# One inference step with retention and experts: the sample tokens' halves in one operand, and their state work placed later in the next head

## What is computed

```python
h = rmsnorm(x, g_mix)
z = h @ w_in                       # 1024 x 4608
u, q, k, v, ga, gb = split(z)      # 512 | 512 | 512 | 1024 | 1024 | 1024
pool_out = windowed mean of u per group, minus u, then w_pool
qf, kf = rotary(q), rotary(k) * 128 ** -0.5
# retention, 4 heads, dk 128, dv 256, chunks of 128 tokens:
#   o = (q k^T * decay) v + (q s) * xi ;  s = g_chunk * s + (k * zeta)^T v
# a sample token is a chunk of one: s_new = gamma * s + k v^T, o = q s_new
mixed = sigmoid(ga) * pool_out + sigmoid(gb) * head_group_norm(ret)
x = x + mixed @ w_out
x = x + hier_moe(rmsnorm(x))       # 32 experts, top 2
y = rmsnorm(x, g_final)
```

## Time and profile before

| | us |
|---|---|
| median of 3 runs | 1100.17 |
| lowest, highest | 1098.19, 1101.92 |
| the profiled execution | 1098.83 |
| its span, first to last instruction | 1096.6 |
| busy: TensorE, its weight loads | 1011.7, 861.0 |
| busy: VectorE, ScalarE, GpSimd | 757.9, 442.1, 203.7 |

### The profile page before, as it was taken

How to read it: one execution, slowest core, us unless ns; L and a number is a source line. 1 busy time by engine, 2 the same in 40 slices (tenths; PEclk the granted TensorE clock), 3 DMA queues, 4 the chain that set the end, 5 groups by cost and what they waited for, 6 DMA issues and landing times.

```text
span 1096.6 us, 17147 instructions
## 1 busy us (share of the span) xinstructions
PE 1011.7 (92%) x5426; PEld 861.0 (79%) x5427; DVE 757.9 (69%) x1846; ACT 442.1 (40%) x733; POOL 203.7 (19%) x227
## 2 busy tenths in 40 slices
PE   5799999999999999999998999958999999999970
PEld 4798888988789888898885888847888777878760
DVE  5675556755557565675556666678999889888955
ACT  6421113011130211301112222136888878978864
POOL 0001220012200122001220000012442322332420
PEclk9899999999999999999998999978999999999995
DMA  8511016010160100701007433289999999999728
GB/s 262 199 29 59 10 38 183 19 59 11 40 190 11 51 19 25 205 12 38 32 19 255 160 154 117 97 348 356 361 383 388 383 384 344 365 378 359 259 27 316
DMA packets 74735, 190.36 MB, mean 174 GB/s; under 512 B 12503, under 2 KB 47555, under 8 KB 62227
## 3 DMA queue, kind: packets, MB, share of 16 engines
q1 hardware_dynamic: 61403, 159.66, 39.5%
q0 software_dynamic: 13248, 29.62, 9.7%
HBM read 167.43 MB, written 38.68 MB: 188 GB/s over the span
## 4 chain that ended last, share of the span: by engine, by line
PE 64%; DMA 23%; DVE 6%; issue 4%; ACT 1%; SPq 1%; POOLq 0%; DVEq 0%; ACTq 0%; POOL 0%
DMA sum_d<-y,icol 19%; PE bank L1790 18%; PE bank L1791 9%; PE bank L848 8%; PE bank L821 5%; PE bank L823 5%; PE bank L822 5%; PE bank L877 1%; PE bank L1813 1%; PE bank L1805 1%; PE bank L1801 1%; PE bank L1685 1%; PE bank L1809 1%; DMA hc<-const_head_tables_dram 1%; PE bank L1677 1%
## 5 line engine op out<-in xcount | busy, mean ns | idle before, releaser
L1194 DVE TENSOR_TENSOR w_lo<-w,w_hi 128x1024 fp32r<-128x1024 f32 x128 | 150.5, 1217 | 0.4 <-DVE vec L1157 0.2
L711 ACT ACTIVATE w_hi<-w 128x1024 fp32r<-128x1024 f32 x128 | 129.4, 1067 | 4.1 <-PE bank L823 4.1
L1790 PE MATMUL bank<-wvg_hi,hT_hi 128*128 128x512 f32 x288 | 117.3, 407 | 0.4 <-DVE kT L1982 0.4
L1790 PE MATMUL bank<-wvg_lo,hT_hi 128*128 128x512 f32 x288 | 113.6, 394 | 0.0
L1790 PE MATMUL bank<-wvg_hi,hT_lo 128*128 128x512 f32 x288 | 113.3, 393 | 0.0
L1638 ACT ACTIVATE v<-bank 128x256 f32<-128x256 f32 x36 | 13.8, 382 | 233.5 <-PE bank L1791 233.5
L821 PE MATMUL bank<-w_hi,xT_hi 128*128 128x512 f32 x256 | 103.6, 405 | 3.3 <-issue 1.4
L823 PE MATMUL bank<-w_hi,xT_lo 128*128 128x512 f32 x256 | 101.0, 394 | 0.0
L822 PE MATMUL bank<-w_lo,xT_hi 128*128 128x512 f32 x256 | 100.5, 393 | 0.0
L821 PE MATMUL bank<-hT_hi,wuqk_hi 128*128 128x344 f32 x288 | 95.9, 333 | 2.7 <-issue 1.8
L2092 POOL TENSOR_TENSOR mixed<-onorm,pgate 128x256 f32<-128x256 f32 x36 | 36.1, 1004 | 314.5 <-DVE onorm L1938 314.5
(11 more groups left out here) (231 smaller groups left out, 2339.5 us busy)
## 6 DMA issues: line engine op xcount, KB each, us to landing
w<-in_w_dram SPq DMA_DIRECT2D x96, 1024.0 KB, 9.3
raw<-in_w_in_dram SPq DMA_DIRECT2D x60, 256.0 KB, 3.3
xall<-in_x_prompt_dram SPq DMA_DIRECT2D x8, 512.0 KB, 6.2
mixed_d<-mixed POOLq DMA_DIRECT2D x32, 128.0 KB, 2.2
sample_state<-in_state_ret_dram SPq DMA_DIRECT2D x16, 256.0 KB, 3.9
out_dram<-sample_state SPq DMA_DIRECT2D x16, 256.0 KB, 3.7
mixed_in<-mixed_d SPq DMA_DIRECT2D x8, 512.0 KB, 4.3
x_again<-in_x_prompt_dram SPq DMA_DIRECT2D x8, 512.0 KB, 3.4
```

What stands on the lines that cost most here:

```text
L711: act.activation(hi, whole_w, ACT.Copy).then_inc(S["up_hi"], 1)
L1194: dve.tensor_tensor(lo, whole_w, hi, ALU.subtract).then_inc(S["up_lo"], 1)
L1790: g = pe.matmul(gates, x[xi], wvg[wi][:, 1:3, k, :], start=first, stop=last)
```

## The change

- `hs`, a new tile, holds for each of eight k-slices the samples' high part at column 88 and the low part at column 120 of a window of 128 columns; windows start 20 columns apart, so other slices' values fall on unused columns. Chunk 8 takes one such window as stationary operand against high and low weights: two pairs of matmuls a slice for three. Rows 88 to 95 of the result (high) and 120 to 127 (low) are then added on VectorE, for v and for the gates.
- The outer products: k is transposed from `kw`, four copies of the last 32 columns; `ks` has k's low part in rows 32 to 63 and its high part in the others, `vs` has v's low part in rows 0 to 31 and high parts in the others, and `kblk` has 128 rows, all in fp32r. One fp32r matmul of 128 rows sums the parts.
- TensorE's loop over heads 1 to 3 is written out.
- The samples' work starts at n = 1 (outer products 0, 1), goes on at n = 3 (pooling product, read 0, outer product 2), n = 4 (read 1, outer product 3), n = 5 and 6 (reads 2 and 3). VectorE updates groups 0 and 1 behind the first three pieces, group 2 behind the rotation of n = 3, group 3 behind that of n = 4; the last three pieces go behind n = 5, the samples' norm behind n = 6 and n = 7.
- SyncE loads pieces 6 to 8 ahead of the wait for the state, and stores and loads sample states in another order among the pieces.

```diff
+HSTEP = 20
+HS = 120 + HSTEP * KT
...
-    m[:, KMASK:KMASK + NB] = i[:, None] == 120 + np.arange(NB)[None, :]
+    m[:, KMASK:KMASK + NB] = i[:, None] % 32 == 24 + np.arange(NB)[None, :]
...
+        def sample_cols(which):
+            at = 88 + 32 * which
+            return hs[:, at:at + HSTEP * KT].rearrange("p (k n) -> p k n", k=KT)[:, :, 0:NB]
...
             def tail(h, between):                      # SyncE
                 between(0)
+                sp.wait_ge(S["state_new"], after(8 * h + 8))
+                carried(sp, "sp")
+                sp.dma_start(ret_p[0, 0, bass.ds(h, 1)].rearrange("a d v -> (a d) v"), state[:, :])\
+                    .then_inc(st_out, 16)
+                between(1)
                 store_states(h, 0)
-                between(1)
                 store_states(h, 1)
+                between(2)
                 load_states(h, 2)
-                between(2)
                 load_states(h, 3)
                 between(3)
...
                     if c < CH:                         # ScalarE
                         act.activation(vb[c % 2][:, :], banks[2 + c % 2][:, 0:DV], ACT.Copy).then_inc(S["v_ev"], 1)
...
+                    else:
+                        act.activation(vs[64:P, :], banks[2][64:P, 0:DV], ACT.Copy)
+                        act.activation(vs[32:64, :], banks[2][64:Q3, 0:DV], ACT.Copy).then_inc(S["v_ev"], 1)
+                        act.wait_ge(S["gates_sum"], after(h + 1))
+                        act.activation(sg[0][Q3:P, :], sg[0][Q3:P, :], ACT.Sigmoid).then_inc(S["sig_done"], 1)
...
-                        mm = pe.matmul(banks[2 + g % 2][:, i * DV:(i + 1) * DV], kblk[Q3:P, 2 * g + i, :],
-                                       vb[0][Q3:P, :], start=True, stop=True)
+                        mm = pe.matmul(banks[2 + g % 2][:, i * DV:(i + 1) * DV], kblk[:, 2 * g + i, :], vs[:, :],
+                                       start=True, stop=True)
...
-                if n == 0:
+                if n == 1:
                     pe.wait_ge(S["kblk_done"], after(h + 1))
...
-                elif n <= 4:
-                    if n == 1:
+                elif 3 <= n <= 6:
+                    if n == 3:
...
-                    read(n - 1)
-                    if n <= 2:
-                        grow(n + 1)
+                    read(n - 3)
+                    if n <= 4:
+                        grow(n - 1)
...
+                    if c == CH:
+                        gates = gates[:, :].rearrange("p (a n) -> p a n", a=2)
+                        for k in range(KT):
+                            x = hs[:, HSTEP * k:HSTEP * k + P]
+                            for wi in range(2):
+                                first, last = k == 0 and wi == 0, k == KT - 1 and wi == 1
+                                g = pe.matmul(gates, x, wvg[wi][:, 1:3, k, :], start=first, stop=last)
+                                m = pe.matmul(v[:, 0:DV], x, wvg[wi][:, 0, k, :], start=first, stop=last)
...
-            with pe.Fori(1, H) as h:
+            for h in range(1, H):
                 head(h, False)
...
+                    lows(0)                            # VectorE
+                    update(h - 1, 0)
+                    update(h - 1, 1)
+                    lows(1)
+                    lows(2)
...
+                    if n in (3, 4):
+                        update(h - 1, n - 1)
+                    elif n == 5:
+                        lows(3)
+                    elif n == 6:
                         finish(h - 1, CH)
+                        now_columns()
+                    elif n == 7:
                         finish_rest(h - 1, CH)
...
+                        steps.do(dve.scalar_tensor_tensor(out=ks[32:64, :], in0=banks[4][32:64, 0:P], scalar=P ** -0.5,
+                                                          in1=ks[32:64, :], op0=ALU.mult, op1=ALU.subtract))
+                        dve.tensor_tensor(kblk[:, :, :], ks[:, :].unsqueeze(1).to_broadcast([P, NB, P]),
+                                          misc[:, KMASK:KMASK + NB].unsqueeze(2).to_broadcast([P, NB, P]), ALU.mult)
...
+                        steps.do(dve.tensor_copy(sg[0][Q3:P, :], banks[1][64:Q3, :]))
+                        dve.wait_ge(S["v_ev"], after(9 * h + 9))
+                        dve.tensor_tensor(vs[0:32, :], banks[2][64:Q3, 0:DV], vs[64:Q3, :], ALU.subtract)\
+                            .then_inc(S["kblk_done"], 1)
+                        dve.tensor_tensor(sg[0][Q3:P, :], sg[0][Q3:P, :], banks[1][Q3:P, :], ALU.add)\
+                            .then_inc(S["gates_sum"], 1)
```

More of the change, by code:

```diff
@@ L228, in step_kernel @@
         wp = rb.place("wp", [P, DV], F32)
-        wp_raw = rb.place("wp_raw", [P, DV], F32)
+        wp_raw = nc.alloc_sbuf_tensor_at("wp_raw", [P, DV], F32, offset=rb.where["qx0"])
+        hs = rb.place("hs", [P, HS], F32R)
         ps_b = rb.place("ps_b", [P, DV], F32)
@@ L907, in stage_c_pe @@
             out_product(0, range(3))
-            for n in range(2, 5):
+            for n in range(4, 7):
                 last_samples(n)
@@ L1500, in head @@
                              uout[15:P:16, 1, :]).then_inc(u_out, 16)
-                sp.wait_ge(S["state_new"], after(8 * h + 8))
-                carried(sp, "sp")
-                sp.dma_start(ret_p[0, 0, bass.ds(h, 1)].rearrange("a d v -> (a d) v"), state[:, :])\
-                    .then_inc(st_out, 16)
             head(0, True, False)
@@ L1581, in between_u @@
                     high_group(2, range(KT))
+                    act.wait_ge(S["zeroed"], after(2))
+                    act.wait_ge(S["h_hi"], after(3 * KT))
+                    act.activation(sample_cols(0), hT[0][:, :, SEQ:NTOK], ACT.Copy)
                     for q in range(6, 16):
@@ L1759, in before @@
                     pe.wait_ge(S["kz_ev"], after(9 * h + c))
-                    at = c * P if c < CH else LAST
+                    at = c * P
+                    if c == CH:
+                        pe.wait_ge(S["scm_done"], after(8 * h + 8))
+                        pe.transpose(banks[4][:, 0:P], kw[:, :], ident).then_inc(S["kt_mm"], 1)
+                        return
                     pe.transpose(banks[4][:, 0:P], kT[:, at:at + P], ident).then_inc(S["kt_mm"], 1)
-                    if c == CH:
-                        return
                     if c == 0:
@@ L1900, in between_qk @@
                     low_group(2, range(KT))
+                    dve.wait_ge(S["h_lo"], after(3 * KT))
+                    dve.tensor_copy(sample_cols(1), hT[1][:, :, SEQ:NTOK])
                     low_first(6)
@@ L1938, in finish_rest, with update @@
                 dve.tensor_tensor(onorm[r, :], onorm[r, :], sgn[s][r], ALU.mult).then_inc(S["on_ready"], 1)
-            def tail(h, between):
-                n = steps.n
-                for g in range(4):
-                    dve.wait_ge(S["skv_mm"], after(4 * h + g + 1))
-                    dve.wait_ge(ss_in[g % 2], 32 * h + 16 * (g // 2) + 16)
-                    dve.scalar_tensor_tensor(
-                        out=sst[g % 2][:, :, :], in0=sst[g % 2][:, :, :], scalar=head_col(2),
-                        in1=banks[2 + g % 2][:, :].rearrange("p (a n) -> p a n", a=2), op0=ALU.mult, op1=ALU.add)\
-                        .then_inc(S["s_upd"], 1)
-                    between(g)
-                assert steps.n == n
+            def update(h, g):
+                dve.wait_ge(S["skv_mm"], after(4 * h + g + 1))
+                dve.wait_ge(ss_in[g % 2], 32 * h + 16 * (g // 2) + 16)
+                dve.scalar_tensor_tensor(
+                    out=sst[g % 2][:, :, :], in0=sst[g % 2][:, :, :], scalar=head_col(2),
+                    in1=banks[2 + g % 2][:, :].rearrange("p (a n) -> p a n", a=2), op0=ALU.mult, op1=ALU.add)\
+                    .then_inc(S["s_upd"], 1)
             def head(h, first, last):
@@ L1982, in head @@
                     dve.tensor_tensor(dst[:, at], dst[:, at], rot[:, :], ALU.add).then_inc(S["qk_ev"], 1)
-                    if n == 3 and not first:
+                    if first:
+                        continue
+                    if n in (3, 4):
[3 more added lines that the diff above has]
+                    elif n == 6:
                         finish(h - 1, CH)
-                    if n == 6 and not first:
+                        now_columns()
+                    elif n == 7:
                         finish_rest(h - 1, CH)
@@ L2063, in lows @@
                     low_mixed(dve, 0)
-            tail(H - 1, lows)
+            for g in range(4):
+                update(H - 1, g)
+                lows(g)
             finish(H - 1, CH)
```

58 lines of the change are left out of this document (34 added, 24 removed).

## The result

| | before | after |
|---|---|---|
| median of 20 runs, us | 1102.49 | 1112.62 |
| lowest, highest | 1098.19, 1111.38 | 1107.00, 1116.37 |
| profiled execution (span) | 1098.83 (1096.6) | 1112.92 (1110.8) |
| mean granted clock of TensorE | 0.967 | 0.952 |

The changed kernel is 0.9% slower, a small difference but one clear of the noise: the ratio is 1.0091, with a 95% interval of 1.0074 to 1.0109. The forecast was 1110.4.

What follows compares the result with a forecast made beforehand. TensorE, busy 92% of the span, was taken as the bound. Savings of 26.1 us against 8.7 for late weights, 22.5 for `hist` waits and 5.1 for clock gave +10.2: 1110.4 us against the median, range 1095 to 1122.

Steps and rivals of the forecast that it cites:

- sample chunk: Projection of the samples on TensorE: 16 matmul pairs for 24 in each of four heads, saving 11.3 us.
- outer products: Products of k and v between heads: eight fp32r matmuls for 16 float32 passes, saving 9.0 us in three boundaries.
- loop gaps: Turns of TensorE's loop over heads: gap and low clock gone once written out, saving 4.8 us.
- waits ahead of the `hist` group: Ahead of product n = 3, TensorE waits for late weights: 2.0, 4.7 and 2.0 us, costing 8.7.
- wait for the `hist` group: At the `hist` transposition TensorE waits for loads issued behind sample-state stores: 7.5 us three times, costing 22.5.
- low clock: TensorE at half speed after each of three `hist` waits: 1.7 us lost each, costing 5.1.
- start of stage C, and behind: At the end SyncE loads `mixed_in` without waiting for the state: saves 1.0 us, bounds 0 and 2.7.
- The lead of the update: VectorE's fourth sample-state update ends 1.9 us before TensorE reaches the `hist` transposition.
- VectorE is late in the same place: At the final `mixed_in` load, reason for taking a gain of 1.0 us where TensorE had waited 2.68.
- Rival B: Short links: `hist` wait of 6.2 us a boundary, 2.7 in part one, no clock loss; 1095 us, chance 0.17.
- C: At the `hist` transposition the loads land in time and savings remain: 1083 us, chance 0.18.
- D: In the boundaries VectorE, without slack, delays more than seen: 5 us a boundary more, 1125 us, chance 0.07.

Runs made afterwards that it cites:

- runs 1 and 2: Early loads of the `hist` group in the changed kernel (1090.11 us) and in the one before (1102.13); u evictions ahead of roundings (1103.0); both edits (1078.05).
- a_both_pad: Changed kernel with early `hist` group loads and early u evictions, plus eight extra matmul pairs in the sample chunk: 1086.24 us, ratio 0.9863.
- a_best_f32: a_both with third state pair loaded ahead of pieces 12 to 14, their remainders behind the third update, and `kblk`, `ks`, `vs` in float32: 1084.48 us.
- b_unroll_both: Kernel before with the loops over heads of TensorE and VectorE both written out: 1096.39 us, ratio 0.9956.
- a_early: Changed kernel with `hist`, `wp_raw` and `ps_b` loaded ahead of the sample states' stores and loads: 1090.11 us, ratio 0.990.
- a_both: Changed kernel with early `hist` group loads and the u evictions ahead of the roundings: 1078.05 us, ratio 0.9812.
- a_both_loop: a_both with TensorE's loop over heads put back: 1082.28 us, ratio 0.9821.
- a_ufirst: Changed kernel with ScalarE's second and third u evictions ahead of rounding pieces 9 to 11 and 12 to 14: 1103.0 us, ratio 1.0013.
- a_unspread: a_both with the samples' work ordered as in the kernel before (outer products from n = 0, updates ahead of rotations): 1096.96 us, ratio 0.9951.
- b_unroll: Kernel before with TensorE's loop over heads alone written out: 1103.03 us, ratio 1.0007.
- b_early: Kernel before with `hist`, `wp_raw` and `ps_b` loaded ahead of the sample states' stores: 1102.13 us, ratio 1.0018.

## Why the prediction was right

Its mechanism is shown by runs 1 and 2, and the total agrees: +10.2 us forecast, +10.1 by the medians. That it agrees so closely is in part luck, since several terms were off and made up for each other: the wait for `hist` came out 5.5 us smaller, the low clock 8.8 larger. Against the span of before (+14.2 us):

| term | forecast | measured |
|---|---|---|
| sample chunk | -11.3 | -9.4 |
| outer products, loop gaps, in three boundaries | -13.8 | -16.9 |
| waits ahead of the `hist` group | +8.7 | +8.5 |
| wait for the `hist` group | +22.5 | +17.0 |
| low clock (what the boundaries take beside idle time) | +5.1 | +13.9 |
| start of stage C, and behind | -1.0 | +1.0 |
| sum | +10.2 | +14.1 |

- **Sample chunk.** T of the first head came 1.8 us earlier, and the three heads behind take 87.8, 87.8 and 87.4 us from project(0) to T for 90.2. The work saved is the 11.4 us of `a_both_pad`; 2 us of it don't arrive: 0.3 us in each of the three later heads stand ahead of the scores of chunk 1, and 1.0 stands ahead of the first `hist` transposition, which starts at 61.3 us for 60.4. That start lies anywhere from 59.9 to 63.1 us in the fourteen traces, so this 1.0 is no more than their scatter.
- **Outer products.** 9.0 forecast, 7.6 by `a_best_f32` (three times 2.5). The boundary without waits fell from 45.86 (`b_unroll_both`) to 42.03, so 1.3 us a boundary came on top; the 32-row operand explains 0.9 of it (1.92 us against 1.54 for the first eight passes, 1.06 against 0.78 for each four behind).
- **Loop.** The size was right as a difference of boundaries, the attribution wrong: "Straight code runs without such gaps in head 0, so I count it all" took the whole difference for TensorE's. Written out alone it gains nothing in the kernel before; it needs VectorE's too (5.4 us in the boundaries). In the changed order the turn shows no gap at all.
- **Weights.** The wait ahead of n = 3 was forecast at 2.0, 4.7 and 2.0 and measured at 1.87, 3.15 and 2.31 us; the second boundary has 1.22 more for a sample state ahead of the read of n = 3. In the first boundary all came some 0.8 us later than forecast, T too (156.6 for 155.6): the load of piece 9 at 167.38 for 166.5, the end of ScalarE's eviction at 173.9 for 173.2, TensorE at 172.1 for 171.2.
- **`hist` group.** The lead of the update was 2.0 us for 1.9. The chain behind it took 8.2, 7.7 and 7.4 where 9.4 was assumed, from rows with two stores outstanding. The mis-sized term is this chain; the waits were 6.1, 5.7 and 5.3 us for 7.5. The section of the Trainium skill that the forecast weighed (DMA: Bandwidth & Descriptors, section Anatomy of one DMA) is headed for transfers that GpSimd issues, and these are SyncE's; the estimate from its figures was 4.5. The measurement lies between that and the rows.
- **Clock.** This term was mis-sized most. It took only the waits for `hist`, and 1.7 us for each, from a row behind 6.48 us of idle time. In fact these cost 2.7, 1.7 and 2.8, and the shorter waits, which the forecast gave nothing, 6.8 in three boundaries.
- **Stage C.** Forecast as a gain of 1.0, it became a loss of 1.4 (T to the output product 13.6 us for 12.2): TensorE waits 3.2 us for the samples' gates, which now go through VectorE first, and 1.9 for the norm of chunk 7. The step "VectorE is late in the same place" was seen, but not costed.
- **Slips in the sums.** The VectorE operations of part one add up to 159.9 and not 160.1; by the earlier trace rows, whose clock for 38 to 39 us is 0.55, the clock was back at 38.9 and not 38.6, 1.8 us lost for 1.7; 2 us of waiting in C's case give 1089 and not 1090; a wait of 4.5 us gives +1.2 and not +1.3; the range leaves out the bounds of the stage C term, 1 to 2 us. None of them changes a choice.

Rival B had 6.2 a boundary for the wait and no clock loss; the wait was near it, the clock was not. C, that the loads land in time, fell. Its case is the one that `a_early` makes by moving them, at 1090 us for C's 1083; of the difference, 5.5 us are slow time behind the waits for n = 3, which C gave nothing. D, 5 us a boundary more, fell too: the boundaries were 22.6 us longer for the forecast's 22.5.

## What to carry to other kernels

When work is spread over a later stretch, list what its queue holds behind it: three small loads with no need of that work stood behind the stores' landing, and this turned a change worth 1.0% into a loss of 0.9%. A saving on the busiest engine is bound by the next engine's order, and a gap of one engine can hide that of another, so take both away before a term is called worthless or real. Cost a wait with the clock behind it, and give it a range: here 25.6 us of idle time cost 39.5, but single waits of one length cost nothing or 1.7.

## What was not expected of the hardware

- Waits of about 2 us bring low clock too: behind 1.87 us of idle time TensorE ran product n = 3 in 5.5 us for 4.0, with 0.58 of its clock granted. Behind 1.63 us in `a_both` and 1.67 in `a_both_loop` it had all of it, behind 1.72 in `a_ufirst` 0.65 of it over 4.9 us, and behind three waits of 1.8 us in `a_unspread` 1.00, 0.57 and 1.00. So no rule of the length alone is drawn from them.
- The turn of TensorE's loop costs 1.0 to 1.8 us of idle time in the kernel before (0.67 + 1.12 and 0.32 + 0.66) and none in `a_both_loop`. That of VectorE's loop cost 2.70 us there, 2.95 in `b_unroll` and 4.01 in `b_early`.
- A float32 pass of 256 columns took 0.24 us with 32 stationary rows and 0.19 with 128.
